# Where the out weights are split into their two float32r parts: hybrid decoder step, one core

## The reference

```
h = rmsnorm(x) * (1 + scale(c)) + shift(c)
z = h @ w_in                                   # 1024 -> 3840, cut into 14 parts
a = pool_mix(pu);  c = cb * conv3(cc * ch)     # trailing means 2/4/8/16; a short convolution
b = mix over dilations 1, 4, 16 of a band attention (6 heads of 64, 129 keys back)
d = band attention (4 query heads, 2 kv heads, sinks, 129 keys back)
y = concat(a, b, c, d) * silu(gates)           # width 1152
out = rmsnorm(x + gate(c) * (y @ w_out)) * final_g
```

## Time and profile before

| | |
|---|---|
| median of 3 runs | 1407.05 us (1403.38 to 1408.56) |
| profiled execution | 1402.11 us |
| its span | 1400.4 us, 21555 instructions |
| mean granted TensorE clock | 0.971 of full speed |
| busy: PE, PEld | 1293.5 us (92%), 1136.5 us (81%) |
| busy: DVE, ACT, POOL | 692.6 us (49%), 468.5 us (33%), 312.9 us (22%) |
| DMA over the span | 214.66 MB, 153 GB/s |

### The profile page before, as it was taken

How to read it: one execution, slowest core, us unless ns; L and a number is a source line. 1 busy time by engine, 2 the same in 40 slices (tenths; PEclk the granted TensorE clock), 3 DMA queues, 4 the chain that set the end, 5 groups by cost and what they waited for, 6 DMA issues and landing times.

```text
span 1400.4 us, 21555 instructions
## 1 busy us (share of the span) xinstructions
PE 1293.5 (92%) x7821; PEld 1136.5 (81%) x7821; DVE 692.6 (49%) x1867; ACT 468.5 (33%) x1220; POOL 312.9 (22%) x402
## 2 busy tenths in 40 slices
PE   4769999999999998999999999879998979999996
PEld 0669999999999997999999877667776648877774
DVE  1771122100244555232321567856878457887883
ACT  1750000121111011122211466657778531333331
POOL 0330000000111122111000035885725301111121
PEclk8799999999999999999999999999999979999999
DMA  8343121211335344369942999842924374555531
GB/s 347 123 177 123 45 90 52 82 75 60 121 121 196 122 141 144 95 161 229 243 137 62 308 266 314 271 141 67 284 85 149 113 224 125 172 160 179 153 128 46
DMA packets 121786, 214.66 MB, mean 153 GB/s; under 512 B 13796, under 2 KB 70533, under 8 KB 118478
## 3 DMA queue, kind: packets, MB, share of 16 engines
q1 hardware_dynamic: 106246, 161.04, 37.3%
q0 software_dynamic: 15456, 52.56, 11.5%
HBM read 136.34 MB, written 77.35 MB: 153 GB/s over the span
## 4 chain that ended last, share of the span: by engine, by line
PE 60%; issue 16%; POOL 7%; DVE 6%; DMA 5%; ACT 4%; SPq 2%; POOLq 0%; DVEq 0%; ACTq 0%
PE psum L1080 16%; PE psum L1081 16%; PE psum L1082 15%; PE psum L1218 3%; PE psum L1191 2%; PE psum L1202 2%; POOL dec_prod L935 2%; PE psum L1192 2%; DMA dil_v_p<-kv_nat 1%; DMA ada_w<-w_ada 1%; POOL resid L1016 1%; DVE logits L1841 1%; PE psum L1227 1%; POOL dec_prod L947 1%; ACT probs L1475 1%
## 5 line engine op out<-in xcount | busy, mean ns | idle before, releaser
L1080 PE MATMUL psum<-h_hi,w_hi 128*128 128x416 f32 (+3 forms) x1224 | 429.3, 351 | 19.7 <-DVE h_lo L1561 10.0
L1081 PE MATMUL psum<-h_lo,w_hi 128*128 128x416 f32 (+3 forms) x1224 | 426.1, 348 | 0.0
L1082 PE MATMUL psum<-h_hi,w_lo 128*128 128x416 f32 (+3 forms) x1224 | 424.6, 347 | 0.0
L1080 PEld LDWEIGHTS psum<-h_hi,w_hi 128*128 128x128 f32 x1224 | 232.8, 190 | 25.6 <-issue 7.8
L1081 PEld LDWEIGHTS psum<-h_lo,w_hi 128*128 128x128 f32 x1224 | 232.9, 190 | 1.3
L1082 PEld LDWEIGHTS psum<-h_hi,w_lo 128*128 128x128 f32 x1224 | 232.6, 190 | 1.2
L1475 ACT ACTIVATE probs<-logits,stats 128x256 f32<-128x256 f32 (+1 forms) x352 | 162.3, 463 | 95.0 <-DVE stats L1841 88.8
L1841 DVE CUSTOM_DVE_ANT_0 logits<-psum,bias_dil 128x256 f32<-128x256 f32 (+1 forms) x288 | 93.5, 362 | 69.2 <-PE psum L1192 55.0
L1080 PE MATMUL psum<-wo_hi,y_hi 128*128 128x512 f32 x288 | 116.8, 406 | 11.7 <-DVE y_lo L1910 11.6
L1082 PE MATMUL psum<-wo_hi,y_lo 128*128 128x512 f32 x288 | 114.0, 396 | 0.0
L1081 PE MATMUL psum<-wo_lo,y_hi 128*128 128x512 f32 x288 | 113.6, 395 | 0.0
(11 more groups left out here) (262 smaller groups left out, 1893.0 us busy)
## 6 DMA issues: line engine op xcount, KB each, us to landing
w_raw<-w_tiles POOLq DMA_DIRECT2D x30, 512.0 KB, 5.0
k_both<-k_dram SPq DMA_DIRECT2D x12, 1024.0 KB, 8.1
q_both<-q_dram SPq DMA_DIRECT2D x20, 512.0 KB, 7.6
mix_dram<-o_st POOLq DMA_DIRECT2D x36, 264.0 KB, 4.9
mix_in<-mix_dram SPq DMA_DIRECT2D x16, 594.0 KB, 4.0
gate_dram<-main SPq DMA_DIRECT2D x9, 1024.0 KB, 4.5
ada_w<-w_ada SPq DMA_DIRECT2D x8, 1024.0 KB, 13.4
x_in<-x_prompt SPq DMA_DIRECT2D x16, 512.0 KB, 4.5
```

Of the source, the lines that this page charges most:

```text
L1080: pe.matmul(out, hi, mhi, start=start, stop=False)
L1081: pe.matmul(out, hi, mlo, start=False, stop=False)
L1082: return pe.matmul(out, lo, mhi, start=False, stop=stop)
```

## The change

The nine chunks go out of the attention stage. In each of the projection tiles 2 to 7 one sixth of `w_out` (128 x 1536) is loaded into a free slot, ACT copies its high part, POOL subtracts for the low part, and SP stores both parts to a DRAM scratch, waits until they have landed, and only then stores the tile's own result. In the attention stage the low parts are fetched by three DMAs of 1.5 MB once POOL's last score is there, and the high parts by three more once the values of unit 127 are weighed; that wait now stands in SP's list, ahead of the loads of the samples' cached values. PE waits for the six DMAs before the first output product. DVE's wait at step 155 goes. In `walk` tiles 0 to 7 stand unrolled. A semaphore is saved by using another link for one small DVE operation. In the diff the hunks stand in the order: scratch and slots, walk, SP, POOL, PE, ACT, DVE.

```diff
+        wo_dram = scratch("wo_dram", [2, P, Y * D])
...
+        WOC = Y * D // 6
+        wo_raw = Plan(slot_at + 3 * SLOT).put("wo_raw", [P, WOC])
+        wo_part = Plan(slot_at + 4 * SLOT).put("wo_part", [P, WOC], F32R)
...
-            for t in (0, 1):
+            for t in range(8):
                 body(t, t // 2, t, "plain")
-            with eng.Fori(0, 3) as i:
-                for b in range(2):
-                    body(2 + 2 * i + b, 1 + i, 2 + b, "plain")
...
+        WO_TILES = range(2, 8)
...
+            def wo_parts(i):
+
+                cols = slice(WOC * i, WOC * i + WOC)
+                sp.wait_ge(gate_mm, 3)
+                sp.dma_start(wo_raw[:], wo_cols[:, cols]).then_inc(wo_raw_loaded, 16)
+                sp.wait_ge(wo_split, i + 1)
+                sp.dma_start(wo_dram[0][:, cols], wo_part[:].bitcast(F32)).then_inc(wo_stored, 16)
+                sp.dma_start(wo_dram[1][:, cols], wo_raw[:]).then_inc(wo_stored, 16)
+                sp.wait_ge(wo_stored, 32 * (i + 1))
...
+                if ts in WO_TILES:
+                    wo_parts(t - 2)
                 sp.wait_ge(bank_free[4], t + 1)
...
             sp.wait_ge(dec_s_ready, 2)
-            for k in range(Y):
-                if k >= 2:
-                    sp.wait_ge(wo_split, k - 1)
-                sp.dma_start(wo_raw[k % 2][:], w_out[:, k, :]).then_inc(wo_loaded[k % 2], 16)
+            for k in range(0, Y, 3):
+                sp.dma_start(wo_lo[:, k:k + 3, :].rearrange("p k e -> p (k e)").bitcast(F32),
+                             wo_dram[1][:, D * k:D * k + 3 * D]).then_inc(wo_loaded, 16)
+            sp.wait_ge(pv_done, LAST)
+            for k in range(0, Y, 3):
+                sp.dma_start(wo_hi[:, k:k + 3, :].rearrange("p k e -> p (k e)").bitcast(F32),
+                             wo_dram[0][:, D * k:D * k + 3 * D]).then_inc(wo_loaded, 16)
...
+                if ts in WO_TILES:
+                    pool.wait_ge(wo_hi_ready, t - 1)
+                    nc.gpsimd.tensor_tensor(wo_raw[:], wo_raw[:], wo_part[:].bitcast(F32), ALU.subtract).then_inc(
+                        wo_split, 1)
...
-            pe.wait_ge(wo_split, Y)
+            pe.wait_ge(wo_loaded, 16 * 6)
...
+                if ts in WO_TILES:
+                    act.wait_ge(wo_raw_loaded, 16 * (t - 1))
+                    nc.scalar.copy(wo_part[:], wo_raw[:]).then_inc(wo_hi_ready, 1)
...
-                if s == LAST + 2:
-                    act.wait_ge(pv_done, LAST)
-                if s % 2 == 0 and LAST + 8 <= s <= LAST + 2 * Y + 6:
-                    weights((s - LAST) // 2 - 4)
...
                 if s == 27:
-                    dve.wait_ge(wo_split, Y)
...
-                if s % 2 == 0 and LAST + 10 <= s <= LAST + 2 * Y + 8:
-                    weights((s - LAST) // 2 - 5)
```

More of the change, by code:

```diff
@@ L217, in build_program @@
         raw_at = bp.at
-        wo_raw = [bp.put(f"wo_raw{b}", [P, D]) for b in range(2)]
+        bp.at += 2 * D * 4
         attention_at = bp.at
@@ L323, in build_program @@
         q_ready = sem("q_ready")
-        wo_loaded = [sem(f"wo_loaded{b}") for b in range(2)]
+        wo_raw_loaded = sem("wo_raw_loaded")
         wo_hi_ready = sem("wo_hi_ready")
         wo_split = sem("wo_split")
+        wo_stored = sem("wo_stored")
+        wo_loaded = sem("wo_loaded")
         fg_loaded = sem("fg_loaded")
@@ L345, in build_program @@
         out_link = sem("out_link")
-        sink_negated = sem("sink_negated")
         unit_open = sem("unit_open")
@@ L686, in first_pieces @@
                     load_piece(sp, 0, j)
+            wo_cols = w_out.rearrange("p k e -> p (k e)")
+            def wo_parts(i):
[6 more added lines that the diff above has]
+                sp.wait_ge(wo_stored, 32 * (i + 1))
             def store(t, half, ts, kind):
@@ L1430, in _ @@
             walk(act, evac)
-            def weights(k):
-                act.wait_ge(wo_loaded[k % 2], 16 * (k // 2 + 1))
-                nc.scalar.copy(wo_hi[:, k, :], wo_raw[k % 2][:]).then_inc(wo_hi_ready, 1)
             def decode(s):
@@ L1688, in opening @@
                 dve.wait_ge(kv_t, len(TURNS))
-                dve.tensor_scalar(neg_sink[:], neg_sink[:], -1.0, None, ALU.mult).then_inc(sink_negated, 1)
-                dve.wait_ge(sink_negated, 1)
+                link(dve.tensor_scalar(neg_sink[:], neg_sink[:], -1.0, None, ALU.mult))
                 pair_tables(0, 0)
```

## The result

The changed kernel takes 1396.24 us (median of 8 runs, 1394.39 to 1400.75), the kernel before 1407.76 us beside it (8 runs, 1403.38 to 1409.12). The ratio is 0.9934, with a 95% interval of 0.9913 to 0.9955: 9.3 us gained, 6.3 to 12.2 (the two medians lie 11.5 us apart). Two further comparisons of the same two kernels gave 0.9937 [0.9916, 0.9958] and 0.9924 [0.9902, 0.9945]. The forecast was 1399.0 us and a gain of 8.1.

A forecast was written before the change was run, and what follows sets the result against it. PE's own work was taken as the bound, with time won only where PE waits or runs slowly. Gains 1.56 + 1.1 + 2.1 + 3.3 = 8.1 us turned 1407.05 into 1399.0 us, range 1393.5 to 1407.5.

The forecast's parts named there:

- The wait of ACT: Steps 130 to 134: ACT's wait for unit 127 goes, gain 1.56 us, bounds 0.5 to 1.69.
- Copies and subtractions: Steps 134 to 150: ACT's copies and DVE's subtractions go, gain 1.1 us, bounds 0 to 1.35.
- the chunk's wait: Steps 150 to 154: the wait for the last weight chunk goes, gain 2.1 us, bounds 0 to 2.4.
- The clock: Steps 154 to 162: without the stall PE's clock doesn't fall, gain 3.3 us, bounds 0 to 5.2.
- DVE's clearing: Step 155: the 1.14 us clearing meets a PE that hasn't stood, charged 0.5 us, 0 to 1.5.
- the same stall need not cost this in every execution: Pair 2: clock falls anyway or median runs hadn't the fall; 4.8 us remain, 1402.2 us, chance 0.18.
- The rule by which I judged: PE clock: falls came with PE busy under 2.7 of 5 us; with 3.50 it stayed at 1.00.
- Projection: Tiles 2 to 7: each part's split chain takes 19.0 us against 22.4 for a tile, cost 0.
- The rival built on it: Projection: chain longer than a tile, PE waits from 26.0 us; at 29, 1416.9 us; chance 0.09 including anything unseen.
- The fetch: Attention: 9.4 MB take 28 us from 1022.2, due 100 us later; cost 0, bounds 0 to 8 us.
- the gain was not hidden: Pair 2: rival that stalls reappear at the clearing and exponents, perhaps 1 us won, 1406 us, chance 0.12.
- no new wait came into pair 2: Pair 2: rival that late o_st stores make ACT stand, some 8 us back, 1407 us, chance 0.06.

The follow-up runs named there:

- both waits moved: Kernel before, with a third raw buffer for the out weights and ScalarE's wait for unit 127 six units later: ratio 0.9955 to the kernel before.
- third buffer: Kernel before, with a third raw buffer for the out weights, each load waiting for the split three chunks earlier: ratio 0.9977 to the kernel before.
- version with GpSimd: Kernel before, with a third raw buffer, ScalarE's wait six units later, and the nine subtractions on GpSimd two steps later: ratio 0.9992 to the kernel before.
- slow chain: Changed kernel, with the store of each part's low half repeated three times, each awaited by SyncE: 1400.33 us, ratio 0.9968 to the kernel before.

## Why the prediction was right

*The wait of ACT:* 1.56 us forecast, 1.88 came, 1.78 of it by moving the wait alone. That is more than the upper bound of 1.69, which took PE's busy time as fixed; it fell too, from 7.75 to 7.41 us.

*Copies and subtractions:* 1.1 forecast for steps 134 to 150, 1.44 came, and both waits moved left 1.37 of it. Here, too, the bound (1.35) failed by PE's busy time, which fell by 0.25 us. I gave the gain to ACT and DVE together; the runs show that it is DVE's. I had not charged the two anywhere else, though: another 1.0 us of them lay behind step 150, within what I booked on the chunk's wait (2.1 forecast, 2.12 came, but the buffer alone gives 1.51) and on the clock. So the 2.1 is right in part by luck: about 0.6 us of the 2.12 came from ACT's copies, which I had not charged there.

*The clock:* this is the term most mis-sized: 3.3 us forecast, 3.90 came, 3.48 of it with the third buffer alone. The 0.5 us charged for DVE's clearing was not there: the clearing takes 1.14 us as before, and PE stands 0.38 us at the turn-out ahead of it, in the changed kernel:

```profile
1079.13 0.65 PE L1252 MATMUL psum<-consts,o_t 128*128 128x128 f32 x4 [0.38 <-ACT o_t L1476]
```

The cause I named is shown: the fall goes with the third buffer and comes back with six copies on ACT. Of twelve profiled executions (all but that of the version with GpSimd), three had a stall at the turn-out of step 154 of 1.71, 2.42 and 3.62 us, and in all three the clock fell; nine had at most 0.99 us there, and in none it fell.

The rival, that the same stall need not cost this in every execution, is right elsewhere. At the turn-out of step 70 PE stood alike in two executions of the changed kernel, in the first and in the one beside the version with GpSimd:

```profile
923.95 0.66 PE L1252 MATMUL psum<-consts,o_t 128*128 128x128 f32 x4 [2.35 <-ACT o_t L1476]
923.95:929.00 5.05, 5.05 (x46) 4.20 (x48) 3.28 (x12) 2.15 (x9) 4.38 (x5) 1.00 0.23 61
921.01 0.66 PE L1252 MATMUL psum<-consts,o_t 128*128 128x128 f32 x4 [2.12 <-ACT o_t L1476]
921.00:926.00 5.00, 4.99 (x34) 4.08 (x36) 2.31 (x10) 2.27 (x10) 4.25 (x5) 0.66 0.43 86
```

The longer stall left the clock at 1.00, the shorter one did not. That agrees with what the Trainium skill says (TensorE: Matmul & The Clock Gate, Part 1), that the monitor's own clock makes the place of the switch vary from run to run. So the 3.3 us were not as sure as the sum had them. For the timed runs the interval decides: without the fall in the kernel before, 5.4 us would have been left of the 9.34, and the gain was 6.3 us or more.

The rule by which I judged was not sound either. I went by PE's busy time in 5 us, under 2.7 before each fall and 3.50 without one; the version with GpSimd fell after a stretch with 3.81 us, and the changed kernel itself ran on at 1.00 through one with 2.65, the one about step 70:

```profile
920.00:925.00 5.00, 2.65 (x25) 2.24 (x26) 2.09 (x8) 4.14 (x15) 4.09 (x9) 1.00 0.91 191
```

The conclusion survived because almost no idle time was left.

*Projection:* the chain was forecast at 19.0 us and took 19.8; its terms erred in both directions (the copy 1.48 against 1.6, POOL 3.49 against 3.6, the two stores 7.4 from the first issue against 5.9). Tiles keep 22.4 us. The rival built on it had the wrong form, as the slow chain shows: I let ACT's weight copy be "due a tile later" and summed the slack at the main buffers, when the copy is where a late part reaches PE first.

*The fetch:* hidden, as forecast, but the stores landed later than the estimate from packets. Issued from 1028 to 1045 us they took:

```profile
DMA to landing us min/median/max: 8.0/8.5/8.9
```

My estimate of 5.7 us rested on what the Trainium skill says of an engine switching between rings after each packet (DMA: Bandwidth & Descriptors, Queues, rings and completion order), with one row of 12 KB put before each packet of the store; no run shows what stood there. The measurement decides, and it is nearer to the 9.3 of the earlier trace rows. The margin to the 12.8 us after which ACT needs the buffer was 3.9 us, not 7.

*The rivals:* in the changed kernel the clock did not fall in steps 130 to 162, the gain was not hidden, no new wait came into pair 2, and behind step 162 the intervals are the same (10.0, 11.28, 11.74 us). The sum of 8.1 us against 9.3 is low by 0.6 at the clock, mainly the clearing's 0.5, and by some 0.3 in each of the first two stretches.

## What to carry to other kernels

Before work is moved off a stage, see whether it is the work or the way it is fed that costs: here two waits and the clock fall behind one of them were 6.85 of 9.34 us, to be had with one more buffer and a wait placed six units later. Price a stall of TensorE with what follows it: stalls of 1.7 to 3.6 us at one turn-out brought 3.5 to 6.3 us more at the lower clock, though at another a stall of 2.35 us brought nothing. For a chain that hangs on several in-order engines, follow what is queued behind each of its waits; the first late consumer needn't be the one at the chain's end.

## What the runs showed of the hardware

At the turn-out of step 154, stalls of 0.38, 0.89 and 0.99 us left the clock at 1.00; stalls of 1.71, 2.42 and 3.62 us went with a fall to 0.50, as did one of 1.19 us at step 150. The length does not decide alone: at step 70, 2.35 us left the clock at 1.00 and 2.12 us did not. What else decides is open. The mean clock over steps 154 to 162 was 0.60, 0.67 and 0.56 behind the three, so the shortest did not cost the least.

Some operations of VectorE ended only behind a subtraction of GpSimd, as if they had waited for it. In the slow chain four of VectorE's 128x1024 subtractions began while GpSimd subtracted; they took 3.70, 3.68, 3.70 and 2.23 us, and each ended 1.08 or 1.09 us behind GpSimd's. The other five of these tiles, with nothing beside them, took 1.23 us, as all do in the changed kernel, where none meets a subtraction of GpSimd:

```profile
259.58 3.50 POOL L901 TENSOR_TENSOR wo_raw<-wo_raw,wo_part 128x1536 f32<-128x1536 f32 x1 [25.47 <-ACT wo_part L1440]
260.47 3.70 DVE L1596 TENSOR_TENSOR w_lo<-w_raw,w_hi 128x1024 fp32r<-128x1024 f32 x1 [14.76 <-ACT w_hi L1400]
```

In the version with GpSimd two operations with two inputs of 32x1 took 1.71 and 0.90 us, against 0.15, and ended 0.02 us behind GpSimd's, while VectorE's copies out of PSUM kept their 0.69 us beside them. I had looked for this only as a rival; it is one more reason why the split on GpSimd fits the projection, where VectorE is busy for 4.22 of 22.42 us, and not the attention.
